# The token load on ScalarE's queue instead of SyncE's, in a two-layer hybrid trunk

## What is computed

```
h = rmsnorm(x, p['norm1_g']) * (1 + sc1) + sh1
u, q, k, v, z, xbc, dt_raw = split_sizes(h @ p['w_in'], IN_SIZES)
# three mixers in parallel: pooling, differential attention, Mamba-2 scan
# gates from h, branch projections, one output projection
x = x + g1 * out
# second norm with sc2, sh2, then a gated feed-forward with a depthwise convolution
x = x + g2 * ffn
```

## Time and profile before

| what | value |
|---|---|
| median of 3 runs | 1292.94 us (1292.47 to 1293.12) |
| the profiled execution | 1292.74 us |
| its span in the profile | 1290.9 us |
| busy: PE, DVE, ACT, POOL | 99%, 84%, 50%, 15% of the span |
| SP's queue (q1) | 56224 packets, 199.38 MB |
| ScalarE's queue (q10) | 144 packets, 0.20 MB |
| GpSimd's queue (q0) | 4016 packets, 15.39 MB |

### The profile page before, as it was taken

The page is one execution under the profiler, slowest core; times in us unless marked ns, Lnnn a source line. Parts: engine busy times, 40 slices in busy tenths (PEclk is TensorE's granted clock), DMA queues, the critical chain, the costliest instruction groups (busy, mean ns, idle before and its releaser), DMA issues.

```text
span 1290.9 us, 20336 instructions
## 1 busy us (share of the span) xinstructions
PE 1272.4 (99%) x7704; PEld 1227.6 (95%) x7704; DVE 1084.3 (84%) x1996; ACT 651.0 (50%) x1098; POOL 196.6 (15%) x191
## 2 busy tenths in 40 slices
PE   7999999999999999999999999999999999999997
PEld 5999899999999999999999988999999999999997
DVE  6899978788988999999969998877988799999433
ACT  5633555655565554443374336654455754544432
POOL 0269100002200000001104950000040000000110
PEclk9999999999999999999999999999999999999999
DMA  9566446444533454457735662564445354544441
GB/s 362 201 229 212 148 139 218 167 148 131 164 130 131 133 170 155 147 191 273 234 120 168 227 210 84 178 230 149 137 126 194 93 168 132 166 139 161 152 127 57
DMA packets 60482, 216.26 MB, mean 168 GB/s; under 512 B 7105, under 2 KB 9409, under 8 KB 58849
## 3 DMA queue, kind: packets, MB, share of 16 engines
q1 hardware_dynamic: 56224, 199.38, 46.1%
q0 software_dynamic: 4016, 15.39, 3.8%
q10 hardware_dynamic: 144, 0.20, 0.0%
HBM read 211.17 MB, written 3.77 MB: 166 GB/s over the span
## 4 chain that ended last, share of the span: by engine, by line
PE 87%; DVE 7%; ACT 3%; issue 1%; DMA 1%; SPq 1%; DVEq 0%; ACTq 0%
PE acc L1052 27%; PE acc L1054 26%; PE acc L1053 26%; DVE wl L1827 2%; DVE junk_front L1916 2%; PE mixes L1322 1%; DMA head<-in_whead_dram 1%; PE mixes L1256 1%; ACT th L1452 1%; ACT hh L1441 1%; PE mixes L1226 1%; PE acc L984 0%; PE mixes L1238 0%; ACT cv L1452 0%; PE misc L1342 0%
## 5 line engine op out<-in xcount | busy, mean ns | idle before, releaser
L1052 PE MATMUL acc<-hh,wh 128*128 128x384 f32 x1519 | 516.2, 340 | 0.5 <-DVE wl L1827 0.2
L1054 PE MATMUL acc<-hh,wl 128*128 128x384 f32 x1519 | 507.8, 334 | 0.0
L1053 PE MATMUL acc<-hl,wh 128*128 128x384 f32 x1519 | 507.7, 334 | 0.0
L1827 DVE TENSOR_TENSOR wl<-raw,wh 128x1024 fp32r<-128x1024 f32 (+1 forms) x276 | 343.3, 1245 | 62.4 <-ACT wh L1416 60.5
L1416 ACT ACTIVATE wh<-raw 128x1024 fp32r<-128x1024 f32 (+1 forms) x276 | 286.7, 1041 | 138.2 <-PE acc L1054 135.8
L1052 PEld LDWEIGHTS acc<-hh,wh 128*128 128x128 f32 x1519 | 285.2, 188 | 8.8 <-issue 3.4
L1053 PEld LDWEIGHTS acc<-hl,wh 128*128 128x128 f32 x1519 | 285.3, 188 | 1.5
L1054 PEld LDWEIGHTS acc<-hh,wl 128*128 128x128 f32 x1519 | 285.1, 188 | 0.0
L2008 DVE SCALAR_TENSOR_TENSOR cv<-acc,prm,cv 128x1 f32<-128x1 f32 (+1 forms) x416 | 153.5, 410 | 7.9 <-ACT cv L1579 0.8
L1052 PE MATMUL acc<-ah,wh 128*128 128x384 f32 x352 | 117.7, 334 | 0.0
L1054 PE MATMUL acc<-ah,wl 128*128 128x384 f32 x352 | 117.6, 334 | 0.0
(11 more groups left out here) (324 smaller groups left out, 1687.0 us busy)
## 6 DMA issues: line engine op xcount, KB each, us to landing
raw<-in_wstream_dram SPq DMA_DIRECT2D x248, 512.0 KB, 3.6
rawm<-in_wstream_dram SPq DMA_DIRECT2D x80, 512.0 KB, 4.3
raw<-in_wstream_dram SPq DMA_DIRECT2D x32, 448.0 KB, 3.5
head<-in_whead_dram SPq DMA_DIRECT2D x8, 1024.0 KB, 15.7
rowf<-runs_dram POOLq DMA_DIRECT2D x12, 256.0 KB, 4.2
rowb<-runs_dram POOLq DMA_DIRECT2D x12, 256.0 KB, 4.8
crow_late<-in_cvec_rows_dram POOLq DMA_DIRECT2D x2, 1024.0 KB, 6.3
crow<-in_cvec_rows_dram POOLq DMA_DIRECT2D x2, 1024.0 KB, 5.4
```

The costliest lines, as they stand in the source:

```text
L1052: mm(out, sh, mhi, start=start, stop=False)
L1053: mm(out, sh, mlo, start=False, stop=False)
L1054: return mm(out, sl, mhi, start=False, stop=stop)
L1827: tt(wl[:, s, 0:n], raw[:, raw_slot(u), 0:n], wh[:, s, 0:n].bitcast(F32), ALU.subtract).then_inc(lo_done, 1)
```

## The change

The two transfers that fill `x` are taken out of SP's program, where they stood between `load_head(0)` and `load_head(1)`, and put ahead of ScalarE's first wait. Destination, source, sizes and the semaphore stay as they are.

```diff
@@ -696,8 +696,6 @@
                     .then_inc(head_in[j], 16)
 
             load_head(0)
-            sp.dma_start(x[:, :, 0:LAT], xs).then_inc(x_in, 16)
-            sp.dma_start(x[:, :, CTX0:T], xp).then_inc(x_in, 16)
             load_head(1)
             for i, (l, kind, u) in enumerate(STREAM):
                 if i == JOINT:
@@ -1707,6 +1705,8 @@
                     last.then_inc(zrs_done, 1)
 
 
+            act.dma_start(x[:, :, 0:LAT], xs).then_inc(x_in, 16)
+            act.dma_start(x[:, :, CTX0:T], xp).then_inc(x_in, 16)
             act.wait_ge(cs_half, 1)
             af(cst[:, :], csh[:, :], ACT.Tanh).then_inc(cs_tanh, 1)
             act.wait_ge(x_in, 32)
```

## The result

The changed kernel takes 1300.65 us (median of 4 runs, 1299.56 to 1301.16) against 1292.70 us for the kernel before, measured beside it. The ratio is 1.0062, with an interval of 1.0050 to 1.0073: 8 us slower. That is inside the predicted range of 1291 to 1313 and on the predicted side of "no change", but 6.7 us under the predicted 1307.3: the loss is little more than half of the 14.6 us that were forecast. The profiled execution took 1300.69 us with a span of 1298.9 us, 8.0 more than the span before.

The account below looks back on a forecast made before the run. TensorE, 99% busy, bounds the kernel, so only S counts: 25.7 (tokens landed) + 8.75 + 1.1 (clock) = 35.55 against 20.98, +14.6 us on 1292.74, giving 1307.3 us; range 1291 to 1313.

Parts of the forecast that it names:

- The two chains that meet at S: Start of kernel: transposes wait for the later of head 2's landing (20.93 us) and X + 8.75; margin 0.15 us.
- S: Start of head 2's transposes on TensorE, 20.98 us before; moving it a microsecond moves the end by one; forecast 35.55.
- X: Landing of the tokens, which ScalarE's squares wait for: about 12.1 us before, forecast 25.7 in the likeliest case.
- Turns by packet: Likeliest case, 0.58: DMA engines alternate packets between both queues, each remaining token packet costing one of SP's; +14.6 us.
- The 25 packets out by 3.0 us: Between 1.6 and 3.0 us, some 25 of each engine's 128 token packets (0.4 MB) go out nearly alone; 1.0 us gained.
- A = 32: Token packets per engine ahead of the turns after 3.0 us, taken midway: 71 paired, 18.9 us, X = 25.7.
- A = 56: Token packets ahead per engine, `crow_late` row read in bytes: 47 paired, 11.2 us, X = 18.0; +5.8 us without the clock.
- The price of the turns: DMA queues from 3.0 us: 71 token packets per engine paired with 71 of SP's, 7.7 MB, 18.9 us.
- The clock: Idle TensorE starts the sums of squares at 1.2 GHz, losing 1.75 us; weight copies cover 0.64; cost 1.1 us.
- The rival in which the clock stays up: TensorE's thin stretch ahead of 20.22 us closes, saving 1.7 us beside the 1.0 gain: 1290.0 us; chance 0.04.
- The issues cost nothing on ScalarE: Two token issues ahead of ScalarE's table load: load ends at 3.32 us, 0.44 us of cover left before the tanh.
- The rival of issue order or equal bytes: Tokens keep their issue place or get equal bytes; head 2 decides at 19.9: -1.0 us, 1291.7; chance 0.30.

Follow-up runs that it names:

- e1: Changed kernel with the prompt tokens loaded by two transfers of 256 B runs, twice the packets, same bytes: 1316.33 us, ratio 1.0180 to the kernel before.
- e4: Changed kernel with 24 unread identity products keeping TensorE busy between the first head and the sums of squares: 1299.28 us, ratio 1.0052 to the kernel before.
- e3: Changed kernel with SP waiting for the tokens to land before it issues head 1: 1294.15 us, ratio 1.0012 to the kernel before.
- e6: Changed kernel with the tokens as one block of 12 KB runs, first on ScalarE's queue: 1293.93 us, ratio 1.0009 to the kernel before.
- e9: Changed kernel with one-block tokens on ScalarE's queue and `tb` issued ahead of them there, `bm` left on SP: 1293.27 us, ratio 1.0000.
- e5: Changed kernel with the 512 B prompt tokens back on SP behind head 0, latent tokens left on ScalarE: 1293.05 us, ratio 1.0002 to the kernel before.
- e8: Changed kernel with the tokens as one block of 12 KB runs, issued by ScalarE behind its tanh: 1294.86 us, ratio 1.0019 to the kernel before.

## Why the prediction was right, step by step

- **The two chains that meet at S** were read rightly. S is X + 8.75 plus the clock: 18.54 + 8.75 = 27.29, and 28.87 was measured. No row of the changed kernel names a head as what TensorE waits for up to there.
- **Turns by packet** was the likeliest case, and it is what happens: equal counts, unequal bytes, and the time follows the number of packets (e1).
- **The 25 packets out by 3.0 us** were wrong. From the first packets up to 3.0 us ScalarE's queue moved 58, which is 3.6 for each engine. The step took the full rate from 1.6 us on, from a half microsecond in which the queue had long been running.
- **A = 32** was a midpoint with no row behind it, and it was too small. With the 25 it put 57 token packets of each engine ahead of the turns; 66 went. The two errors largely offset one another, which is luck. A = 56 gives X = 18.0, close to the 18.54, but by a lead of 81 packets, so that is luck too; the runs don't show that the lead is counted in bytes.
- **The price of the turns** was the term that was mis-sized. The sum paired 71 token packets of each engine with 71 of SP's of 4 and 8 KB, 7.7 MB. In the trace, SP's queue moved 946 packets from 6.0 us on, 59 for each engine, and only 45 of those held 4 or 8 KB; the other 223 in all were under 2 KB, `tb` among them. That is 4.49 MB, 3.2 MB less, some 8 us at the measured 0.40 MB a us. X came 7.2 us earlier than the sum had it (18.5 instead of 25.7); less 0.5 us that the clock took beyond its term, this is the miss of 6.7 us in the total. The rate was right: 5.0 MB of both queues in 12.5 us is 0.40 MB a us, against 0.41. So the mechanism was forecast and the size was not; the wide range held it.
- **The clock**, +1.1, was 1.6 in the trace (28.87 less 27.29), and e4 gives 1.4 to 1.8. The sums lost 2.36 us (7.79 less 5.43) where 1.75 had been forecast. The weight copies covered what had been forecast, 0.64: `rs` waited 1.68 us for the sums. The rival in which the clock stays up falls with this.
- **The issues cost nothing on ScalarE**: the table load ends at 3.39 (3.32 forecast). The tanh is later, 4.92 against 3.76, but because `bm` landed at 4.7 and not because of the issues.
- **What was missed**: the small tables, issued behind the tokens and on the other queue, are held up as well, the first matmul from 4.24 to 7.97. In the changed kernel X hides it. In e3, e6 and e9, where the tokens were early, it set S, 1.1 to 1.6 us later than before, and took the gain from them; in e5 by 0.3 us.
- **The rival of issue order or equal bytes** (1291.7) falls with the 21 to 20 packets. The rule that issuing from several engines saves only issue time (the Trainium skill, page "DMA: Bandwidth & Descriptors", section "Issuing engines are not separate DMA queues") would have given that rival if it is read as "nothing else changes"; here the second queue cost 8 us, so the measurement decides against that reading.

## What to carry to other kernels

Before a load is moved to a second queue, count its packets on each DMA engine and the size of the packets that will stream beside it: once both ran here, each of its packets cost about one of theirs, so the load of short runs beside a stream of long ones landed 6.4 us later though it was issued 2 us earlier. Lengthen the runs first; on the same queue that alone was worth 1.2 us here. And look at what small and urgent was next in line, since a big load that goes earlier pushes that back too.

## What the runs showed of the hardware that was not expected

- A transfer can wait for microseconds although its queue has nothing in front. In e8 the tokens, issued at 3.29 us, moved nothing until 6.8; in the changed kernel `tb`, issued at 1.64, moved nothing until 6.0, with nothing moving on SP's queue from 4.5. Meanwhile the other queue carried 46 to 78 KB of each engine, in 9 to 80 packets. Transfers issued within 0.01 us of each other took turns from the start (e6). The rule stays open.
- A transfer of 57 KB (`bm`, issued at 1.17 us) landed after 2.4 us in the kernel before, after 3.5 in the changed one, and after 6.8 with a block of 12 KB runs issued 0.43 us ahead of it on another queue, where `cs` ahead of it on its own queue had to take turns with that block.
- The tokens' first packets come slowly: 3.6 for each engine by 3.0 us, from a queue whose first transfer was issued at 0.74, against 12 in a half microsecond at 5.0. This isn't so for every first transfer: in e9 `tb`, with runs of 1 KB and issued first on the same queue at 0.73, moved 122 packets by 2.5 us and landed 2.3 us after its issue.
